# Retention's scores and cross product on two row halves, and V products with V stationary on two column halves, in a two-layer float32 decoder trunk

## What is computed

```python
# retention, chunks of 128 tokens
scores = einsum('bhncd,bhnkd->bhnck', qc, kc) * decay
o_inner = einsum('bhnck,bhnkv->bhncv', scores, vc)
def step(R, inp):
    q_n, kz_n, v_n = inp
    o = einsum('bhcd,bhdv->bhcv', q_n, R)
    R = R * chunk_decay + einsum('bhcd,bhcv->bhdv', kz_n, v_n)
    return R, o
# the output is o_inner + xi * o_cross, normed per head and gated

# dilated and window attention
p = exp(s - m)
o = einsum('bhgnqk,bhnkd->bhgnqd', p, vb) / den
```

## Time and profile before

| | us |
|---|---|
| median of 3 runs | 2365.36 (2365.22 to 2365.97) |
| profiled execution | 2364.84 |
| its span, first to last instruction | 2363.1 |
| TensorE busy with products in the span | 2316.7 |
| TensorE's mean granted clock | 0.999 of full |

### The profile page before, as it was taken

The page is one execution under the profiler, slowest core; times in us unless marked ns, Lnnn a source line. Parts: engine busy times, 40 slices in busy tenths (PEclk is TensorE's granted clock), DMA queues, the critical chain, the costliest instruction groups (busy, mean ns, idle before and its releaser), DMA issues.

```text
span 2363.1 us, 34417 instructions
## 1 busy us (share of the span) xinstructions
PE 2316.7 (98%) x12184; PEld 1973.2 (83%) x12184; DVE 1444.8 (61%) x2862; ACT 830.8 (35%) x1701; POOL 1103.5 (47%) x994
## 2 busy tenths in 40 slices
PE   6999999999999999999999999999999999999999
PEld 6888888889978888888887788889978888888887
DVE  6564646462475776577674666662475676577664
ACT  5525243531332233223232555552332233233220
POOL 5323232322174665567464533332184666467461
PEclk9999999999999999999999999999999999999999
DMA  3111111123112111210203111013102210210211
GB/s 128 28 28 28 27 28 28 28 63 94 41 32 72 63 47 32 71 53 18 89 25 114 41 31 30 19 51 103 54 19 72 63 62 18 71 53 23 83 36 72
DMA packets 140981, 120.35 MB, mean 51 GB/s; under 512 B 26048, under 2 KB 126912, under 8 KB 140864
## 3 DMA queue, kind: packets, MB, share of 16 engines
q1 hardware_dynamic: 133488, 103.70, 14.2%
q10 hardware_dynamic: 7376, 15.12, 1.9%
HBM read 110.41 MB, written 8.39 MB: 50 GB/s over the span
## 4 chain that ended last, share of the span: by engine, by line
PE 87%; DVE 7%; POOL 2%; issue 2%; ACT 1%; DMA 1%; SPq 0%; DVEq 0%; ACTq 0%; POOLq 0%
PE gp L483 14%; PE gp L485 13%; PE gp L484 13%; PE sc L485 6%; PE sc L483 6%; PE sc L484 6%; PE o_ps L567 2%; PE tp L484 2%; PE tp L483 2%; PE tp L485 2%; PE sc L546 2%; PE o_ps L603 2%; PE tp L555 1%; PE qt L483 1%; PE qt L485 1%
## 5 line engine op out<-in xcount | busy, mean ns | idle before, releaser
L483 PE MATMUL gp<-W_hi,hT_hi 128*128 128x384 f32 (+1 forms) x1152 | 418.3, 363 | 5.8 <-POOL W_lo L1812 5.5
L485 PE MATMUL gp<-W_hi,hT_lo 128*128 128x384 f32 (+1 forms) x1152 | 381.9, 331 | 0.0
L484 PE MATMUL gp<-W_lo,hT_hi 128*128 128x384 f32 (+1 forms) x1152 | 381.1, 331 | 0.0
L1937 POOL TENSOR_TENSOR W_lo<-af,W_hi 128x512 fp32r<-128x512 f32 x168 | 238.1, 1417 | 282.5 <-ACT W_hi L1094 282.5
L1917 POOL TENSOR_TENSOR W_lo<-raw,W_hi 128x1024 fp32r<-128x1024 f32 x72 | 187.6, 2611 | 230.5 <-ACT W_hi L1036 217.7
L1631 DVE TENSOR_TENSOR af<-af 128x512 f32<-128x512 f32 x112 | 81.2, 725 | 300.5 <-ACT af L1077 300.5
L483 PEld LDWEIGHTS gp<-W_hi,hT_hi 128*128 128x128 f32 x1152 | 218.3, 189 | 40.7 <-issue 31.7
L1937 POOL TENSOR_TENSOR W_lo<-rb,W_hi 128x512 fp32r<-128x512 f32 x168 | 244.2, 1454 | 0.0
L484 PEld LDWEIGHTS gp<-W_lo,hT_hi 128*128 128x128 f32 x1152 | 219.0, 190 | 0.0
L485 PEld LDWEIGHTS gp<-W_hi,hT_lo 128*128 128x128 f32 x1152 | 217.5, 189 | 0.0
L483 PE MATMUL gp<-hT_hi,W_hi 128*128 128x512 f32 x512 | 199.5, 390 | 0.0
(11 more groups left out here) (300 smaller groups left out, 5330.5 us busy)
## 6 DMA issues: line engine op xcount, KB each, us to landing
raw<-in_mlp_w_up SPq DMA_DIRECT2D x64, 512.0 KB, 4.4
rb<-in_mlp_w_down SPq DMA_DIRECT2D x56, 512.0 KB, 5.4
raw<-in_hyb_w_in SPq DMA_DIRECT2D x74, 128.0 KB, 2.4
X<-in_x SPq DMA_DIRECT2D x8, 512.0 KB, 7.5
X<-in_x ACTq DMA_DIRECT2D x8, 512.0 KB, 3.3
raw<-in_mlp_w_down SPq DMA_DIRECT2D x8, 512.0 KB, 3.3
raw<-in_swa_w_qkv SPq DMA_DIRECT2D x16, 256.0 KB, 3.1
x_spill<-X ACTq DMA_DIRECT2D x8, 512.0 KB, 2.6
```

What stands on the lines that cost most here:

```text
L483: mm(o, a[0], b[0], start=first, stop=False)
L484: mm(o, a[0], b[1], start=False, stop=False)
L485: return mm(o, a[1], b[0], start=False, stop=last)
L1937: E.tensor_tensor(WF_lo[:, c], x(k), WF_hi[:, c].bitcast(f32), ALU.subtract).then_inc(op_ready, 1)
```

## The change

- Retention: q and k come out of the projection in the order k, q (`load_R`), and k, q, scaled q and scaled k lie side by side in QK. Two transposes replace three: k alone, and q with scaled q in one of 128 columns. rqT then holds k and q transposed on its lower 64 partitions and scaled q on its upper 64. The state rR and its addition r_add lie on the upper 64 partitions.
- The product with the state moves from `ret_values` to `ret_scores`, where it stands behind the scores, on the array's other row half. With it the waits for r_x and r_R of tile r - 1 move to the head of `ret_scores`, for r >= 1.
- V products: V is the stationary side (64 columns), pT the moving one (128), head 0 writes partitions 0 to 63 of o_ps and head 1 partitions 64 to 127. The output is transposed: ScalarE copies it to SBUF (`part_copy_O`, `copy_O`), TensorE transposes it back into the last quarter of qt (`part_back`, `back`), and VectorE divides from there, half a slot to a slot later than before.
- New waits keep qt's other quarters, QK and o_back from being overwritten: TensorE for o_evac before some transposes into qt, VectorE for qkt_ready and qt_done, POOL for r_st.

The diff, with little context:

```diff
@@ -160,11 +160,10 @@
         rsT = at("rsT", [P, P])
-        rR = at("rR", [HD, 2, RV])
+        rR = at("rR", [P, 2, RV])
         rsg = at("rsg", [P, 2, RV])
         re = at("re", [P, 2, RV])
-        rQK = at("rQK", [P, 2, 2 * HD])
-        rqT = at("rqT", [HD, 3, P])
+        rqT = at("rqT", [P, 2, P])
         off[0] = A0
@@ -214,7 +213,9 @@
         half_out = tp[:, 512:1024]
-        r_add = sc[0:HD, P:P + RV]
+        o_back = qt[:, 3 * P:4 * P]
+        LO, HI = slice(0, HD), slice(HD, 2 * HD)
+        r_add = sc[HI, P:P + RV]
         r_out = sc[:, 512:512 + RV]
@@ -246,6 +247,7 @@
         max_ready = sem("max_ready")
+        ot_copied, ot_done = sem("ot_copied"), sem("ot_done")
         u_done, u_evac, a_sq, a_hi_done, a_ready, d_done, d_evac = [
@@ -279,6 +281,10 @@
             return 0 <= a < T and (c == 0 or a >= 4)
+
+        def o_turned(kind, n):
+
+            return qT[:, n % 2, P:2 * P] if kind == "D" else Pm[:, n % 2, 512:512 + P]
@@ -384,7 +390,7 @@
                 v = 2 * RH * HD
-                runs(w_in[0], [(0, HD, h * HD), (HD, HD, RH * HD + h * HD), (2 * HD, RV, v + h * RV),
+                runs(w_in[0], [(0, HD, RH * HD + h * HD), (HD, HD, h * HD), (2 * HD, RV, v + h * RV),
                                (2 * HD + RV, RV, v + RH * RV + h * RV)], first)
@@ -560,13 +566,24 @@
                 if c == 0 and g * T + a >= 1:
-                    pe.wait_ge(o_evac, g * T + a)
-                for h in range(2):
-                    for x in range(0, part_width(a, c), P):
-                        b = c * 4 + x // P
-                        last = mm(o_ps[:, h * HD:(h + 1) * HD], pT[:, c, h * 512 + x:h * 512 + x + P],
-                                  V[:, b, h * HD:(h + 1) * HD], start=b == h == 0, stop=b == a and h == 1)
+                    pe.wait_ge(ot_copied, g * T + a)
+                for x in range(0, part_width(a, c), P):
+                    for h in range(2):
+                        b, r = c * 4 + x // P, slice(h * HD, (h + 1) * HD)
+                        last = mm(o_ps[r, 0:P], V[:, b, r], pT[:, c, h * 512 + x:h * 512 + x + P],
+                                  start=b == 0, stop=b == a)
                 last.then_inc(pv_done, 1)
+
+            def part_back(g, a):
+                pe.wait_ge(ot_copied, g * T + a + 1)
+                pe.wait_ge(qkt_ready, g * T + min(a + 3, T))
+                nc.tensor.transpose(o_back, o_turned("D", a), ident[:, :]).then_inc(ot_done, 1)
+
+            def back(n, t):
+                pe.wait_ge(ot_copied, A_S + n + 1)
+                pe.wait_ge(qkt_ready, A_S + min(t - 1, NG * T))
+                pe.wait_ge(o_evac, A_S + n)
+                nc.tensor.transpose(o_back, o_turned("S", n), ident[:, :]).then_inc(ot_done, 1)
@@ -597,11 +614,12 @@
                 pe.wait_ge(v_ready, A_S + n // 2 + 1)
-                pe.wait_ge(o_evac, A_S + n)
+                pe.wait_ge(ot_copied, A_S + n)
                 bl = blocks(a)
-                for m, (_, to, c, e) in enumerate(bl):
-                    last = mm(o_ps[:, e * HD:(e + 1) * HD], pT[:, j, to:to + P], V[:, c, 0:HD],
-                              start=(m == 0 or bl[m - 1][3] != e), stop=(m == len(bl) - 1 or bl[m + 1][3] != e))
+                for m in range(len(bl) // 2):
+                    for _, to, c, e in (bl[m], bl[m + len(bl) // 2]):
+                        last = mm(o_ps[e * HD:(e + 1) * HD, 0:P], V[:, c, 0:HD], pT[:, j, to:to + P],
+                                  start=m == 0, stop=m == len(bl) // 2 - 1)
                 last.then_inc(pv_done, 1)
@@ -614,29 +632,25 @@
                 alone(pe)
-                q, k, qx = rQK[:, r % 2, 0:HD], rQK[:, r % 2, HD:2 * HD], QK[:, r % 2, 4 * HD:5 * HD]
-                for m, src in enumerate((q, k, qx)):
-                    last = nc.tensor.transpose(qt[0:HD, m * P:(m + 1) * P], src, ident[:, :])
-                last.then_inc(r_qt, 1)
+                nc.tensor.transpose(qt[LO, 0:P], QK[:, r % 2, 0:HD], ident[:, :])
+                nc.tensor.transpose(qt[:, P:2 * P], QK[:, r % 2, HD:3 * HD], ident[:, :]).then_inc(r_qt, 1)
...
                     pe.wait_ge(sm_ready, (g + 1) * U_D)
+                else:
+                    pe.wait_ge(r_x, n)
+                    pe.wait_ge(r_R, n)
                 pe.wait_ge(r_qtev, n + 1)
-                mm(sc[:, 0:P], rqT[:, 1, :], rqT[:, 0, :], start=True, stop=True)
-                mm(r_add, QK[:, r % 2, 5 * HD:6 * HD], v, start=True, stop=True).then_inc(r_st, 1)
+                mm(sc[:, 0:P], rqT[LO, 0, :], rqT[LO, 1, :], start=True, stop=True)
+                if r >= 1:
+                    mm(r_out, rqT[HI, 1, :], rR[HI, r % 2, :], start=True, stop=False)
+                mm(r_add, QK[:, r % 2, 3 * HD:4 * HD], v, start=True, stop=True).then_inc(r_st, 1)
...
                 pe.wait_ge(r_sT, n + 1)
-                if r >= 1:
-                    pe.wait_ge(r_x, n)
-                o = r_out
-                last = mm(o, rsT[:, :], G[:, r % RING, 2 * HD:2 * HD + RV], start=True, stop=(r == 0))
-                if r >= 1:
-                    pe.wait_ge(r_R, n)
-                    last = mm(o, rqT[:, 2, :], rR[:, r % 2, :], start=False, stop=True)
-                last.then_inc(r_o, 1)
+                mm(r_out, rsT[:, :], G[:, r % RING, 2 * HD:2 * HD + RV], start=(r == 0), stop=True).then_inc(r_o, 1)
@@ -663,6 +677,8 @@
                             if j == 1 and 0 <= r < T:
+                                if t - 5 < T:
+                                    pe.wait_ge(o_evac, g * T + t - 4)
                                 ret_T(r, g * T + r)
@@ -689,7 +705,11 @@
                                 ret_scores(r, g * T + r, g)
+                            if j == (t - 4 >= 4) and 0 <= t - 4 < T:
+                                part_back(g, t - 4)
                             if j == 1 and 0 <= t - 1 < T:
+                                if 0 <= t - 4 < 4:
+                                    pe.wait_ge(o_evac, g * T + t - 3)
                                 heads_T("D", t - 1, g * T)
@@ -722,6 +742,8 @@
                         next(steps)
+                        if 0 <= n - 3 < units:
+                            back(n - 3, t)
                         if j == 1 and 0 <= t - 1 < units // 2:
@@ -912,7 +934,7 @@
                 act.wait_ge(r_qt, n + 1)
-                A(rqT[:, :, :].rearrange("p m c -> p (m c)"), qt[0:HD, 0:3 * P], ACT.Copy).then_inc(r_qtev, 1)
+                A(rqT[:, :, :].rearrange("p m c -> p (m c)"), qt[:, 0:2 * P], ACT.Copy).then_inc(r_qtev, 1)
@@ -933,6 +955,14 @@
                 last.then_inc(p_ready, 1)
+
+            def part_copy_O(g, a):
+                act.wait_ge(pv_done, part(g, a, a >= 4) + 1)
+                A(o_turned("D", a), o_ps[:, 0:P], ACT.Copy).then_inc(ot_copied, 1)
+
+            def copy_O(n):
+                act.wait_ge(pv_done, U_S + n + 1)
+                A(o_turned("S", n), o_ps[:, 0:P], ACT.Copy).then_inc(ot_copied, 1)
@@ -989,6 +1019,10 @@
                                 heads_probs(g, t - 2)
+                            if j == 1 and 0 <= t - 3 < 4:
+                                part_copy_O(g, t - 3)
+                            if j == 0 and 4 <= t - 4 < T:
+                                part_copy_O(g, t - 4)
                             if j == 0 and t in D_SPLIT_AT:
@@ -1018,6 +1052,8 @@
                             probs(n)
+                        if 0 <= n - 2 < units:
+                            copy_O(n - 2)
                         if t >= O1_T:
@@ -1372,6 +1408,8 @@
                 dve.wait_ge(gemm_evac, evac)
+                if r == 0:
+                    dve.wait_ge(qt_done, n + T)
                 if n >= 2:
@@ -1385,13 +1423,12 @@
                 step.wait()
-                q = rQK[:, r % 2, :]
-                step.did(E.tensor_tensor(q, rA, rB, ALU.add))
-                step.wait()
-
-                step.did(E.tensor_scalar(QK[:, r % 2, 4 * HD:5 * HD], q[:, 0:HD], xi[:, bass.ds(h, 1)], None, ALU.mult))
-                E.tensor_scalar(QK[:, r % 2, 5 * HD:6 * HD], q[:, HD:2 * HD], zeta[:, bass.ds(h, 1)], None,
-                                ALU.mult).then_inc(r_qk, 1)
+                k, q, qx, kz = [QK[:, r % 2, m * HD:(m + 1) * HD] for m in range(4)]
+                step.did(E.tensor_tensor(QK[:, r % 2, 0:2 * HD], rA, rB, ALU.add))
+                step.wait()
+
+                step.did(E.tensor_scalar(qx, q, xi[:, bass.ds(h, 1)], None, ALU.mult))
+                E.tensor_scalar(kz, k, zeta[:, bass.ds(h, 1)], None, ALU.mult).then_inc(r_qk, 1)
@@ -1406,12 +1443,12 @@
                                 ALU.mult).then_inc(r_sT, 1)
-                new = rR[:, (r + 1) % 2, :]
+                new = rR[HI, (r + 1) % 2, :]
                 if r == 0:
...
                     dve.wait_ge(r_R, n)
-                    E.scalar_tensor_tensor(new, rR[:, r % 2, :], cdec[0:HD, bass.ds(h, 1)], r_add,
+                    E.scalar_tensor_tensor(new, rR[HI, r % 2, :], cdec[HI, bass.ds(h, 1)], r_add,
```

(24 more changed lines are left out.)

## The result

The changed kernel takes 2404.5 us (median of four runs, 2399.7 to 2405.9) against 2365.3, a ratio of 1.0164 (95% interval 1.0152 to 1.0176): 39 us slower. I had forecast 2384, with a range up to 2400. The direction and the mechanism were right; the size was half, and the time lies outside the range.

What follows compares the result with a forecast made beforehand. TensorE was taken as the bound nearly everywhere, except retention tiles, where VectorE's chain decides. Dilated and retention -12.6 + 3 x 4.5 + 13.9 = +14.8, window +3.0, clock +1: +18.8 on 2364.84, so 2384 us; range 2356 to 2400.

Steps and rivals of the forecast that it cites:

- the ring: Retention tiles: scores wait for the previous tile's VectorE output, which follows rope; 6.75 us per late tile, longer elsewhere.
- Rival (a): Retention: VectorE finishes before TensorE reaches the next scores, so all TensorE savings count; -30.0 us, 2335; chance 0.08.
- Rival (b): V products: column halves don't overlap, 0.213 us more per block, +52.8 us, 2436; chance 0.11.
- V groups and pairing: V products overlap on column halves: 0.57, 0.79, 1.00, 1.21 us for one to four blocks; cross product pairs with scores.
- the far row: V products: full overlap of column halves assumed from L546, a row-half pair, 0.49 us for four passes.
- The ring of the first three heads: Retention tiles 1 to 7: 45.0 us against 40.5 before, +4.5 for each of these heads.
- The last head: Retention tiles 1 to 7: ScalarE's copy delays rope; 60.9 us against 46.95 before, +13.9.
- the clock's term: Last head: TensorE's idle pauses lower its granted clock, mostly falling into slack; 0 to 7 us, taken as 1.
- The heads' boundaries: Between heads, tile 0 to 1: TensorE still has most work, so savings count; last `ret_values` saves 0.63 us more.
- Slots t = 7 and 8: Dilated heads: V-group savings less back transposes counted as gained; -2.7 us per pair over slots 3 to 10.
- The window layer: Sliding-window heads: V products -4.0 us, back transposes +7.0, together +3.0 us.
- a mild form of (b): V products: one pass unpaired in each of 112 groups, adding 12 us, 2396; chance 0.06.

Runs made afterwards that it cites:

- wait_only: Kernel before with only the wait for r_x and r_R of tile r - 1 moved to the head of `ret_scores`, no product moved: 2403.2 us, ratio 1.0155.
- swapped: Changed kernel with retention's halves exchanged, state on the lower 64 partitions, k, q and scores on the upper: 2393.9 us, ratio 1.0116.
- v_only: Kernel before with only the V products on column halves, their copies and back transposes, retention as before: 2361.8 us, ratio 0.9980.
- best: Changed kernel with a second r_out bank, the next tile's gate moved into `ret_out`, and window-layer V products as before: 2346.4 us, ratio 0.9911.

## Why the prediction was right and wrong

**The mechanism: right.** Moving one wait past the projection makes a ring through VectorE. It was shown by the wait alone (37 us), by opening the ring (38 back) and by shortening it (30 back). The ring's length by the prediction's sum, 6.75 us, is that of `wait_only`. Rival (a) is dead: VectorE's chain was over 5.6 us in every interval. Rival (b) is dead as well: column halves overlap.

**V groups and pairing: right to 0.02 us** per group. The choice of the far row (row halves) for an absent shape (column halves) came out well; no row of before bore on it, so it was a guess with a chance, not a reading. The Trainium skill ("TensorE: Matmul & The Clock Gate", Part 3) states that a load overlaps products in flight only when its row group differs. Two column halves share theirs, and here sixteen passes took 1.09 us, with their loads: the measurement decides against it for this shape.

**Where the 16 us of the profiled execution went** that the sum did not hold (34.9 measured, 18.8 forecast):

- *The ring of the first three heads, +6.* Forecast 45.0 us for tiles 1 to 7, measured 47.0, three times. The failed step is the sum of VectorE's operations: I took 6.75 us from the trace of before as if the state's move to the upper 64 partitions cost VectorE nothing, and gave this unseen operation no bound. It cost 0.38 us per tile between tiles 4 and 6 and some 0.3 at the earlier ones; in `swapped` the same tiles take 44.8 to 45.4 us, the forecast's sum again. The rule to bound whatever the trace doesn't show was kept for TensorE's shapes and forgotten for VectorE's operand.
- *The last head, +3.3 beyond the 1 us that the clock's term held.* Forecast 60.9, measured 65.2, +4.3. The term "clock, 0 to 7, I take 1" is mis-sized: with the clock at full but for one stretch it is 61.65. I had the pauses (3.78 us in the trace, 4.7 forecast) and the one row that showed what follows such a pause, and still took a value near the lower end, because "most of the slower work falls into slack". The slow transposes of X lie in the ring, as the same sentence said, and each of three falls cost 0.9 to 1.5 us.
- *The heads' boundaries, +3.7.* The first scores of the next group (L552) write the same bank as r_out and wait for L1463 of the last tile, 1.0 us each at two of the three boundaries. The two slots there take 10.89 us, and 11.45 at the third, where the clock was slow, for 10.48 before, where about 0.6 less was forecast. This order existed before and cost nothing, and in `wait_only` it costs nothing either (no such wait): what uncovers it is that TensorE arrives earlier while VectorE's chain got longer (the runs allow no finer split). `swapped` has 0.7 us of it back (10.19). I searched for what the moved wait holds up, and not for what else waits on r_x.
- *Slots t = 7 and 8, +3.* The savings of two V groups, 0.75 us after the back transposes, didn't come: the two slots take 19.72 us, before 19.67. There the transposes of the probabilities (L561) wait for ScalarE's exponentials (L956, 2.2 us in four cases, 2.5 in `v_only`; none before). In the last group's slots 7 and 8 both sides moved. TensorE has the V group of 1.09 us where it had one of 1.90. And from the last part's scores to the exponentials it is 2.88 us (468.70 to 471.58) where it was 2.26 (453.05 to 455.31): VectorE now makes `heads_outputs` (L1528, L1530, 0.40 us) right in front of that part's maxima, where the change put it, and L1480 before it took 1.92 us instead of 1.52, for a reason that is open. "TensorE is the bound nearly everywhere" was read from a share of busy time, and the later place of `heads_outputs` was priced only in the ring. `v_only` shows it by itself: 4.5 us gained, where the forecast's terms give 8.9.
- *The window layer, +0.3.* +3.0 forecast, 3.3 us from first to last score (281.4 for 278.1); undoing it in `best` gave 2.4 by the traces.

The five add up to 16.4, and what is left nets to -0.3. Each is small for one tile or slot and adds up over 28 tiles, 3 boundaries or 8 slots; all five have one sign. The range failed for that reason: its upper end came from a different case (a mild form of (b)) and the forecast's own case reached only to 2392, as if every operation not named were free. In the sum itself two slips of 0.1 us and less didn't matter: one ring of 11.2 stands in the last head's sum as 11.3, and 6.74 as 6.75.

The remainder between 16 and the nearly 21 us of the medians is the runs' spread: the profiled execution of after is the fastest of its runs (2399.7 to 2405.9).

## What to carry to other kernels

Before an instruction is moved past a long stretch of independent work, follow its waits round: if the releaser itself waits for something behind the new place, there is a ring, and its length, not the engine's load, is the time per tile; what the waiting engine saves inside it is worth nothing, and what the other engine needs more comes in full. Such a ring is repaired cheaply by a second buffer for the output that closes it and by filling the other engine's idle time inside it, and here neither was enough alone. When several small costs are put at nothing, put the sum of them at the upper end of the range: here all five had one sign.

## What the runs showed of the hardware

- Float32 products on two column halves overlapped in full, loads among them (1.09 us for sixteen passes, 1.90 before), and for a two-block group (eight passes) even when four passes for one half stood before four for the other in the program (0.80 against 0.79 us).
- Around the update of the state VectorE's operations overlapped by some 0.08 us with the state on partitions 0 to 63, and not at all with it on 64 to 127: 0.11 us at each hand-over. Statistics behind it lost theirs too when no other operation had read PSUM on the lower partitions since (15 of 32 tiles), and kept it otherwise (17 of 32). Together it is 0.38 us per late tile of the first three heads and some 10 us in the kernel.
- In the last head the granted clock was 0.50 behind TensorE's pauses of 3.78, 3.20 and 2.70 us. With twenty useless transposes in each of five pauses it stayed at 1.00 there, and the head's tiles 1 to 7 took 61.65 us instead of 65.2.
